# Expert rows scattered with accumulation into one row per token

## The reference

```
h  = rmsnorm(x, g) * (1 + sc2) + sh2                      # 512 x 1024
y  = swiglu(h, shared) + moe_routed(h)
x  = x + g2 * y

moe_routed: scores = sigmoid(h @ router_w); top 6 of 64 experts per token, weights normalised, times 2.5
            token's result = sum over its 6 experts of weight * swiglu(h, expert)   # 1024->512->1024
```

## Time and profile before

| | |
|---|---|
| median of three runs | 3247.81 us |
| the profiled execution | 3257.22 us |
| its span | 3255.6 us |
| TensorE busy | 2916.3 us (90%) |
| VectorE busy | 2041.0 us (63%) |
| ScalarE busy | 1568.3 us (48%) |
| GpSimd busy | 609.9 us (19%) |
| DMA, whole span | 673.64 MB, mean 207 GB/s |

### The profile page before, as it was taken

One profiled execution on the slowest core, in us unless ns is written; L12 is line 12 of the kernel. 1 busy time (PEld: TensorE's weight loads), 2 busy tenths in 40 slices (PEclk: granted clock), 3 DMA queues, 4 the chain that ended last, 5 costly groups with the idle time before them and its releaser, 6 DMA issues. The chain is left out here.

```text
span 3255.6 us, 42356 instructions
## 1 busy us (share of the span) xinstructions
PE 2916.3 (90%) x13756; PEld 2217.6 (68%) x13756; DVE 2041.0 (63%) x2874; ACT 1568.3 (48%) x2422; POOL 609.9 (19%) x577
## 2 busy tenths in 40 slices
PE   1799999899979999999669999988998899999994
PEld 1567776577757777777455777766776677777773
DVE  3454445554458888888555444465545788888885
ACT  0333332442337777777423424243323577777770
POOL 0100000000043333333210000000002333333332
PEclk9899999999889999999868999999998899999995
DMA  8123333123349999999531243312324799999975
GB/s 204 59 78 110 125 115 128 54 101 135 117 176 352 367 362 374 356 371 357 190 142 52 92 142 109 135 60 97 116 97 194 262 365 359 360 374 363 358 265 205
DMA packets 120101, 673.64 MB, mean 207 GB/s; under 512 B 27468, under 2 KB 28876, under 8 KB 84972
## 3 DMA queue, kind: packets, MB, share of 16 engines
q1 hardware_dynamic: 87340, 609.85, 50.9%
q0 software_dynamic: 31456, 57.70, 5.3%
q10 hardware_dynamic: 1152, 4.19, 0.3%
HBM read 656.86 MB, written 56.98 MB: 219 GB/s over the span
## 5 line engine op out<-in xcount | busy, mean ns | idle before, releaser
L1838 DVE TENSOR_TENSOR ew_lo<-ew,e_hi 128x2048 fp32r<-128x2048 f32 x260 | 595.8, 2292 | 191.1 <-ACT e_hi L1696 191.0
L698 PE MATMUL bank<-h_hi,w_hi 128*128 128x512 f32 x1248 | 516.6, 414 | 49.3 <-DVE gt L781 18.4
L632 DVE TENSOR_TENSOR w_lo<-raw,w_hi 128x1024 fp32r<-128x1024 f32 x198 | 242.6, 1225 | 492.3 <-ACT w_hi L624 492.1
L1696 ACT ACTIVATE e_hi<-ew 128x2048 fp32r<-128x2048 f32 x260 | 497.3, 1914 | 102.8 <-PE bank L1983 80.5
L698 PE MATMUL bank<-h_hi,w_lo 128*128 128x512 f32 x1248 | 504.2, 404 | 0.0
L698 PE MATMUL bank<-h_lo,w_hi 128*128 128x512 f32 x1248 | 502.7, 403 | 0.0
L1983 PE MATMUL bank<-e_hi,x_hi 128*128 128x512 f32 x1040 | 419.4, 403 | 0.0
L1983 PE MATMUL bank<-ew_lo,x_hi 128*128 128x512 f32 x1040 | 408.2, 392 | 0.0
L1983 PE MATMUL bank<-e_hi,x_lo 128*128 128x512 f32 x1040 | 406.1, 391 | 0.0
L1598 POOL DMA_INDIRECT y_d<-y,idx x128 | 218.7, 1709 | 623.0 <-issue 526.8
L698 PEld LDWEIGHTS bank<-h_hi,w_hi 128*128 128x128 f32 x1248 | 241.1, 193 | 135.9 <-issue 43.0
(11 more groups left out here) (291 smaller groups left out, 4454.2 us busy)
## 6 DMA issues: line engine op xcount, KB each, us to landing
ew<-in_wexp SPq DMA_DIRECT2D x130, 2048.0 KB, 9.8
raw<-in_wmix SPq DMA_DIRECT2D x297, 512.0 KB, 4.0
ew<-in_wexp SPq DMA_DIRECT2D x130, 1024.0 KB, 9.5
yt<-y_d SPq DMA_DIRECT2D x8, 3072.0 KB, 15.5
ada<-in_ada SPq DMA_DIRECT2D x4, 2048.0 KB, 18.0
h_d<-htok ACTq DMA_DIRECT2D x8, 512.0 KB, 2.7
v_d<-vB SPq DMA_DIRECT2D x1, 3840.0 KB
xg<-h_d,idx POOLq DMA_INDIRECT x130, 9.4
```

The source lines that it names most:

```text
L632: nc.vector.tensor_tensor(w_lo[q % SPLIT][:], raw[u % RAW][:], w_hi[q % SPLIT][:].bitcast(F32), ALU.subtract).then_inc(lo_done, 1)
L698: ins = nc.tensor.matmul(out, lhs, rhs, start=start, stop=stop)
L1696: nc.scalar.activation(e_hi[h][:], up_part(ew, j, h), ACT.Copy).then_inc(whi_done, 1)
L1838: nc.vector.tensor_tensor(up_part(ew_lo, j, h), up_part(ew, j, h), e_hi[h][:].bitcast(F32), ALU.subtract).then_inc(wlo_done, 1)
```

## The change

A scatter now adds its rows in memory to one row per token, `ysum_d`. For this the memory is cleared once a layer: GpSimd sets `blank` (in bytes of `merged`), SP stores it four times behind the load of tile 11, and VectorE waits for the stores before it first writes `merged`. Since two experts may have the same token, GpSimd waits for the previous scatter's landing before it issues the next, the overflow blocks' too. The combine loads one row per token, 512 KB for each group into a buffer of its own, and adds nothing up; TensorE uses four banks in place of two, and waits for the add-back two groups before.

```diff
+        blank = place("blank", [P, D], at=m0 + 12288)
-        yt = [place(f"yt{i}", [P, TOPK, D], at=t_end[f"ew{i}"] - 24576) for i in range(3)]
+        yt = [place(f"yt{i}", [P, D], at=t_end["ew1"] - 24576 + 4096 * i) for i in range(TC)]
-        y_d = nc.dram_tensor("y_d", [S * TOPK, D], F32, kind="Internal").ap()
+        ysum_d = nc.dram_tensor("ysum_d", [S, D], F32, kind="Internal").ap()
@@ dve_out, out == "branch"
+                if j.arg == 0:
+                    dve.wait_ge(ysum_set, 16 * TC)
@@ mixer block, sync
                     for u in range(RAW, MIX_TILES):
                         load_tile(sp, l, u)
+                        if u == RAW + 8:
+                            sp.wait_ge(blank_set, 1)
+                            for t in range(TC):
+                                sp.dma_start(ysum_d[t * P:(t + 1) * P, :], blank[:]).then_inc(ysum_set, 16)
+                    sp.wait_ge(ysum_set, 16 * TC)
@@ mixer block, gpsimd
+                    nc.gpsimd.memset(blank[:], 0.0).then_inc(blank_set, 1)
                     nc.gpsimd.memset(tabA[:], 0.0).then_inc(pchain, 1)
@@ expert block, gpsimd, scatter
                         pool.wait_ge(yA, e + 1)
                         pool.wait_ge(yD, e + 1)
+                        if not (isinstance(e, int) and e == 0):
+                            pool.wait_ge(y_out[(j - 1) % 4], 16 * (2 * it + (j - 1) // 4 + 1))
                         pool.sem_inc(settled, 1)
...
                             nc.gpsimd.indirect_dma_start(
-                                out=y_d,
-                                out_offset=bass.IndirectOffsetOnAxis(ap=idx[j % 8][0:n, 1:2].bitcast(U32), axis=0),
-                                in_=y[j % 2][0:n, :], in_offset=None, bounds_check=S * TOPK - 1, oob_is_err=False
-                            ).then_inc(y_out[s], 16)
+                                out=ysum_d,
+                                out_offset=bass.IndirectOffsetOnAxis(ap=idx[j % 8][0:n, 0:1].bitcast(U32), axis=0),
+                                in_=y[j % 2][0:n, :], in_offset=None, bounds_check=S - 1, oob_is_err=False,
+                                compute_op=ALU.add).then_inc(y_out[s], 16)
@@ the overflow scatters in the same way, behind y_out[3] and y_out[0]
@@ combine block, sync
-                        if t >= 3:
-                            sp.wait_ge(ytr, 2 * (t - 2))
-                        sp.dma_start(yt[t % 3][:], y_rows[t * P:(t + 1) * P]).then_inc(yt_in[t % 3], 16)
+                        sp.dma_start(yt[t][:], ysum_d[t * P:(t + 1) * P]).then_inc(yt_in[t], 16)
@@ combine block, gpsimd: the loop of L2070 to L2073 is gone
@@ combine block, vector: the sums of L2099 to L2102 are gone; only add_back is left
                     for t in range(TC):
                         for b in range(2):
                             dve.wait_ge(ytr, 2 * t + b + 1)
                             for k in range(4):
                                 x = xT[:, 4 * b + k, t * P:(t + 1) * P]
-                                ins = nc.vector.scalar_tensor_tensor(x, G[b][:, k * P:(k + 1) * P],
+                                bank = TB[b] if t % 2 else G[b]
+                                ins = nc.vector.scalar_tensor_tensor(x, bank[:, k * P:(k + 1) * P],
                                                                      mod[:, 40 + 4 * b + k:41 + 4 * b + k], x, ALU.mult, ALU.add)
                             ins.then_inc(yadd[b], 1)
@@ combine block, tensor
-                        pe.wait_ge(ysum, t + 1)
+                        pe.wait_ge(yt_in[t], 16)
                         for b in range(2):
-                            if t:
-                                pe.wait_ge(yadd[b], t)
+                            if t >= 2:
+                                pe.wait_ge(yadd[b], t - 1)
+                            bank = TB[b] if t % 2 else G[b]
```

More of the change, by code:

```diff
@@ L421, in hybrid_trunk @@
             sem("o_yA"), sem("o_yD"))
-        yt_in = [sem(f"yt_in{i}") for i in range(3)]
+        yt_in = [sem(f"yt_in{i}") for i in range(TC)]
+        blank_set, ysum_set = sem("blank_set"), sem("ysum_set")
         ysum, ytr, yadd = sem("ysum"), sem("ytr"), [sem("yadd0"), sem("yadd1")]
-        ypair, ysq_ready, ysq_sum, ymean, pre_in = sem("ypair"), sem("ysq_ready"), sem("ysq_sum"), sem("ymean"), sem("pre_in")
+        ysq_ready, ysq_sum, ymean, pre_in = sem("ysq_ready"), sem("ysq_sum"), sem("ymean"), sem("pre_in")
         per_layer = range(min(s.num for s in sems.values()), max(s.num for s in sems.values()) + 1)
@@ L1636, in _ @@
                     pool.wait_ge(yD, NE + 1)
+                    pool.wait_ge(y_out[3], 16 * (NE // 4))
                     pool.sem_inc(settled, 1)
                     nc.gpsimd.indirect_dma_start(
-                        out=y_d, out_offset=bass.IndirectOffsetOnAxis(ap=idx[0][:, 1:2].bitcast(U32), axis=0),
-                        in_=y[0][:], in_offset=None, bounds_check=S * TOPK - 1, oob_is_err=False
-                    ).then_inc(y_out[0], 16)
+                        out=ysum_d, out_offset=bass.IndirectOffsetOnAxis(ap=idx[0][:, 0:1].bitcast(U32), axis=0),
+                        in_=y[0][:], in_offset=None, bounds_check=S - 1, oob_is_err=False,
+                        compute_op=ALU.add).then_inc(y_out[0], 16)
                     nb = blocks(pool)
@@ L1654, in _ @@
                             pool.sem_inc(settled, 1)
+                            pool.wait_ge(y_out[0], 16 * (NE // 4 + 1))
                             nc.gpsimd.indirect_dma_start(
-                                out=y_d, out_offset=bass.IndirectOffsetOnAxis(ap=idx[0][:, 1:2].bitcast(U32), axis=0),
-                                in_=y[0][:], in_offset=None, bounds_check=S * TOPK - 1, oob_is_err=False
-                            ).then_inc(o_put, 16)
+                                out=ysum_d, out_offset=bass.IndirectOffsetOnAxis(ap=idx[0][:, 0:1].bitcast(U32), axis=0),
+                                in_=y[0][:], in_offset=None, bounds_check=S - 1, oob_is_err=False,
+                                compute_op=ALU.add).then_inc(o_put, 16)
                             pool.wait_ge(o_put, 16 * i)
@@ L2052, in _ @@
                             ins.then_inc(o_dn, 1)
-            y_rows = y_d.rearrange("(t k) d -> t k d", k=TOPK)
             with nc.Block() as block:
@@ L2069, in _ @@
                 def _(pool):
-                    for t in range(TC):
-                        v = yt[t % 3]
-                        pool.wait_ge(yt_in[t % 3], 16 * (t // 3 + 1))
-                        nc.gpsimd.tensor_tensor(v[:, 4, :], v[:, 4, :], v[:, 5, :], ALU.add).then_inc(ypair, 1)
                     pool.wait_ge(ymean, 1)
@@ L2087, in _ @@
                 def _(dve):
-                    def add_back(t):
+                    for t in range(TC):
                         for b in range(2):
@@ L2092, in add_back @@
                                 x = xT[:, 4 * b + k, t * P:(t + 1) * P]
-                                ins = nc.vector.scalar_tensor_tensor(x, G[b][:, k * P:(k + 1) * P],
+                                bank = TB[b] if t % 2 else G[b]
+                                ins = nc.vector.scalar_tensor_tensor(x, bank[:, k * P:(k + 1) * P],
                                                                      mod[:, 40 + 4 * b + k:41 + 4 * b + k], x, ALU.mult, ALU.add)
                             ins.then_inc(yadd[b], 1)
-                    for t in range(TC):
-                        v = yt[t % 3]
-                        dve.wait_ge(yt_in[t % 3], 16 * (t // 3 + 1))
-                        link(dve, nc.vector.tensor_tensor(v[:, 0:2, :], v[:, 0:2, :], v[:, 2:4, :], ALU.add))
-                        link(dve, nc.vector.tensor_tensor(v[:, 0, :], v[:, 0, :], v[:, 1, :], ALU.add))
-                        dve.wait_ge(ypair, t + 1)
-                        nc.vector.tensor_tensor(v[:, 0, :], v[:, 0, :], v[:, 4, :], ALU.add).then_inc(ysum, 1)
-                        if t:
-                            add_back(t - 1)
-                    add_back(TC - 1)
                     dve.wait_ge(ysq_sum, TC)
```

5 lines of the change are left out of this document (2 added, 3 removed).

## The result

The changed kernel takes 3330.73 us (median of 4 runs, 3316.79 to 3345.04) against 3248.16 (4 runs, 3247.25 to 3249.17): ratio 1.025, 95% interval 1.0228 to 1.0272. It is slower by 2.5%, where 3224 was forecast. This is the place of rival A, between its two worked figures of 3298 and 3343.

A forecast was written before the change was run, and what follows sets the result against it. TensorE bounds the expert loop, DMA engines close behind; neither bounds the combine. 3257.22 - 47.8 (combine) + 2 (last scatters) + 2 (clearing) + 20 (loops) = 3233.4; less 9.4 to the runs' median: 3224 us, own range 3196 to 3240.

The forecast's parts named there:

- rival A: Expert loop: the chain of waiting scatters becomes the bound; 3298 us at landing 9.0, 3343 at 9.4; chance 0.28.
- The combine: First load to statistic shrinks from 50.4 to 26.5 us, saving 23.9 us a layer, 47.8 in all.
- C: Combine shrinks less because small loads land like the large one, 6.3 us a layer lost; 3247 us; chance 0.04.
- The last scatter: Between loop and combine: its landing stands bare and now reads memory rows too; 0 to 1.9 us, taken as 1 a layer.
- The clearing: Four stores behind tile 11 delay tile 12 and on; 0 to 6.2 us a layer, taken as 1.
- The expert loop: Longer scatter landings and the new wait stall single steps and late gathers; 20 us for both loops, range 0 to 36.
- I take +1.2: Expert loop: what accumulation adds to a scatter's 6.4 us landing, part of the read running beside the load wait.
- low bound of 0: Expert loop: accumulation adds nothing to a scatter's landing, as completion seems to ride on the load queue; loops cost 0.
- The high bound: Expert loop: an accumulating scatter lands in 9.4 us, the gather's median, +3.0 over the plain one.
- (a): Expert loop's scatter chain: a step takes landing + 1.6 us; the plain 6.4 leaves 1.7 of the 9.72 us period.
- (b): Expert loop: the gather queued behind the waiting scatter has only 2.2 us left before TensorE needs its rows.
- B: Expert loop: DMA engines become the bound; 3247 us if scatter packets take twice as long, 3310 if three times; chance 0.10.

The follow-up runs named there:

- e2: Kernel before plus the scatter's addition only, still a row per token and expert, no new wait: 3286.4 us, ratio 1.0122 to before.
- e1: Kernel before plus only GpSimd's wait for the previous scatter's landing, plain scatter without addition: 3294.74 us, ratio 1.0131 to before.
- e10: Changed kernel with rows overwritten instead of added and the expert's row count read before the waits: 3217.89 us, ratio 0.9909 to the kernel before.
- e5: Changed kernel with each gather issued one step earlier: 3276.22 us, ratio 1.0099 to the kernel before.
- e6: Changed kernel with two sum memories, for even and odd experts, and no wait for the previous scatter: 3255.42 us, ratio 1.0029 to the kernel before.
- e7: Changed kernel with two sum memories, no wait for the previous scatter, and each gather one step earlier: 3236.43 us, ratio 0.9962 to the kernel before.
- e4: Changed kernel with rows overwritten instead of added, the wait kept: 3236.76 us, ratio 0.996 to the kernel before.

## Why the prediction was wrong

**The combine** was right: 50.4 to 25.4 and 23.6 us, 51.8 saved where 47.8 were forecast, and by the order worked out, with TensorE's sums as what is late next. C fell: the first group lands in 3.8 us.

**The last scatter** was put at +1 a layer and is +3.3 and +1.6, with its landing 5.9 and 3.3 us where it was 3.1 and 2.2. **The clearing** was put at 1 us a layer; the wait for tile 12 is 1.01, in mixer blocks whose whole length shows nothing of it.

**The expert loop** is where it failed, +125.5 where 20 were put, in three steps.

*The landing was mis-sized.* "I take +1.2" stood between 0 and 3.0; e2 measured +2.7, which is 9.1 + 1.6 = 10.7 for a chain step where 9.2 was put. The reason given, that a part of the read runs beside the wait for the load, and the use made of the Trainium skill (DMA: Bandwidth & Descriptors, Queues, rings and completion order: a completion lands only behind earlier writes of its engine), left out that the loads land later too: 11.4 and 11.6 us in e2 against 9.6 and 9.0. The completion does go with the load: in e2's window 35 of the 56 scatters land within 1.5 us of the down load ahead of them, and the whole queue has become 2 us slower. Most of the others land later, some by over 5 us. No run tells apart how much of the 2.7 is the scatter's own read and how much is the load ahead of it; the low bound of 0 is out either way. The high bound, the landing of a gather that reads as many rows, was the near one.

*A mean step that fits was taken to be safe.* "At 7.6 the mean chain step is 9.2 and fits. Single ones do not": each late scatter was priced once, 2.2 us. e1 refutes this without any addition: its landing was 6.2 us while it ran free, 7.8 with GpSimd's part, below 9.72, and yet it spent twenty experts at a time at 10.4. The landing that was read in the trace before belonged to scatters that start at a fixed place between the loads, 3.5 us behind the down load; a wait moves the start, and in e1 the landing moved with it, from 4.5 to 8.8 us in the two steps shown. In e10, with 0.6 us off the step, the late gait didn't hold.

*The two limits were added, and they feed each other.* (a) and (b) were each priced with the other at rest. In the queue of GpSimd the gather stands behind the waiting scatter, which the prediction names, but its 2.2 us of margin were counted once for the chain and not at every step. e5 gives 54.5 us of the loss back by giving the gather room, e6 75 by taking the wait away; alone the wait costs 33 and the addition 36, together 125.5.

The range had a slip of its own: its terms add up to 3248 - 42 + 3.8 + 12 + 36 = 3258 at the upper end, and 3240 was written; 3330.73 lies outside either.

**Rival A** had the mechanism and the sign, and its total came out near by luck: with the measured 8.7 us its rule gives a step of 10.3 and some 60 us in all, half of the 125.5 measured, since it too leaves out the gathers; its figures of 3298 and 3343 assume longer landings, 9.0 and 9.4. What it had against itself, that a longer period shortens the landing, hardly happened: 8.7 at 322 GB/s against 9.1 at 354 in e2. **B** was right on the engine time (scatters doubled, e2) and not on its effect: at 17.2% TensorE never waited for weights. Its sign shows only in e7, where the loads land after 20 us, and there too TensorE waits for no split weights.

The chance of 0.28 for A was too small on the evidence then in hand. The trace held scatters of 11.4 us in one loop of 9.72, and 1.7 us of room against an unknown of 0 to 3.

## What to carry to other kernels

A wait that strings asynchronous transfers together turns latency into throughput: compare landing plus the issuer's own part with the period, for the long ones as well as for the median, and expect the landing to change once the wait moves the start. Before such a wait is added, look at what is queued behind it on the same engine, and give that room first; or break the chain (two destinations cost one more load and one add in the combine, here 2 to 6 us a layer, and 75 us fewer in all). With the queue that full, a small load that is needed soon must not stand behind large ones (e7). Work done by an accumulating scatter isn't free because no engine does it: it took about twice the DMA engines' time of a plain one, and its landing grew by 2.7 us.

## What the runs showed of the hardware

- An accumulating scatter of the same rows lands in 9.1 us against 6.4 and takes the DMA engines about twice as long, if the gathers' part is unchanged (GpSimd's queue, gathers included, 17.2% against 11.2%), and GpSimd's issue takes 2303 ns against 1850. The bytes that the profile counts don't grow: 57.72 MB of this queue in the whole span, 57.70 without the addition (before and e10), so what the addition costs must be read from the share.
- With the DMA engines at a share of 1.00, 1 and 2 MB loads landed after 20 us while scatters and gathers issued later landed in 10 to 11: GpSimd's transfers were not queued behind SP's, but a 2 KB load of SP's own was (15.4 and 18.9 us). At 1201.25 us in e7 a gather is issued which lands after 10.2; a down load issued 0.03 us later lands after 18.6.
- A loop whose chain of waits is a little below its period ran in two gaits, 9.74 and 10.4 us a step, for twenty steps at a time, in one execution (e1, e4). Where a scatter was issued 3.5 us behind a 1 MB load it landed with that load, after 4.5 us; where it was issued together with the next one it landed with that, after 8.8. In both runs the long late stretches ended behind a stall of TensorE of 5.4 to 7.8 us or with the loop.
